# Feed-forward gate products of a two-layer block: the high weights meet high and low rows in one matmul of 512 columns

## The chip, the cores and the metric

The kernel runs on one core of one Trainium2 chip. The metric is device time in microseconds (us) of one launch; three runs of the kernel before gave 1533.83, 1536.38 and 1536.64 us, median 1536.38 us.

## The reference, cut to what matters

A sequence of 256 tokens with 1024 features goes through two layers. Each layer is feed-forward, token mixing (window attention, a gated recurrence and gated linear attention), feed-forward; each part reads a normalised and modulated copy of x and adds its output to x. Shift, scale and gate come from nine vectors per layer, products of a condition vector with w_ada (1024 x 9216 per layer). All is float32. The part that changes is the first product of the four feed-forwards:

```
def swiglu(h, w_i, w_o):                       # h: 256 x 1024, w_i: 1024 x 5632, w_o: 2816 x 1024
    a, g = jnp.split(h @ w_i, 2, axis=-1)
    return (jax.nn.silu(g) * a) @ w_o
h = modulate(rms_norm(x, norm_g[l, 0]), sh1, sc1)
x = x + 0.5 * g1[:, None, :] * swiglu(h, w_ff_in[l, 0], w_ff_out[l, 0])
```

## The kernel before, in words

Activations are held transposed: 128 features on the partitions, 256 tokens along the row, in C = 8 chunks. Every weight slab is 128 x 2048 floats (eight chunks of 128 x 256). The precision of float32 comes from splitting: ScalarE copies the raw slab to a rounded high part (`hi`, line 1015), VectorE subtracts to get the low part (`lo`, line 1494), and TensorE computes high x high, high x low and low x high, each as a matmul of 256 moving columns (`slab_tile`, line 503). A product of one slab is 2 output tiles x 8 chunks x 3 = 48 matmuls into the two halves of one PSUM bank. There are 240 slabs; three slots hold split slabs, so `hi` of slab p waits until slab p - 3 has been multiplied. SyncE loads the raw slabs into four slots.

A feed-forward handles 11 blocks of 256 hidden features, called rounds 0 to 10 here (`j` in the code); the four feed-forwards are called F1 to F4 (norms 0, 2, 3 and 5 in the code). TensorE's order in a round j is: gate product of block j+1 (bank 4), down product of block j (banks 0 to 3, 48 matmuls), up product of block j+1 (bank 5). In the last two rounds up 10 comes before down 9. ScalarE applies Silu to bank 4 (line 1088), VectorE multiplies by bank 5 (line 1633), ScalarE rounds the result (line 1111), VectorE takes its low part (line 1637), and only then may the down product begin. The order of each engine is written out by hand:

- VectorE in round j: `lo` of gate j+1; multiply j; `lo` of down j; low part of hidden j; `lo` of up j+1; then `weigh` (below). The next round begins with `lo` of gate j+2.
- ScalarE in round j: `hi` of gate j+1; `hi` of down j; high part of hidden j; `hi` of up j+1; Silu of gate j+1.
- TensorE waits for `lo` of a slab before its product, for Silu j before gate j+1 (bank 4 is used again), and for multiply j before up j+1.

Beside this, VectorE computes the modulation vectors: `weigh` multiplies and adds four 128 x 512 pieces of w_ada (lines 1384 and 1390), `fold_block` transposes and reduces every second one (lines 1401 and 1405). How many halves a round gets is a table, `FF_HALVES = [0, 2, 2, 1, 1, 1, 1, 2, 2, 0, 0]`; F4 has only the first four halves, in rounds 1 and 2. TensorE finishes the vectors in `ada_group` (line 601, bank 7): one at round 8, and in F1 to F3 a second one in round 9, after gate 10 and before up 10, which waits until VectorE has copied out the first (`ada_columns`, line 1414, in round 9 after `lo` of down 9). In F1 VectorE also has small operations of a series in rounds 1 to 8 (lines 1444 to 1470).

The first gate and up products of F2 to F4 (`lead`, banks 4 to 7) and gate 1 (`rows_halves`) have their own forms, and so have those of F1 (`stage`). In the opening, the first blocks of modulation (`ada`, line 587) go to banks 6 and 7 in turn.

Of the kernel before, what the change touches and what calls it, by code (L numbers as in the profile page):

```python
# [8 lines left out]
F32R = mybir.dt.float32r  # L9
# [5 lines left out]
P = 128  # L15
DEPTH = 2
D = 1024
T = 256
# [87 lines left out]
def build(nc, x, c, w_ada, b_ada, norm_g, w_ff_in, w_ff_out, w_in, qk_norm_g, attn_sinks, rel_bias,  # L106
# [3 lines left out]
    with ctx:  # L110
# [3 lines left out]
        def sem(name):  # L114
# [12 lines left out]
        h_hi, h_lo = sb("h_hi", [C, T], F32R), sb("h_lo", [C, T], F32R)  # L127
# [89 lines left out]
         consts_ready, bias_masked, fold_ready, ada_folded, ma_ready, mhi_ready, mlo_ready, xhi_ready, xlo_ready, lead_scaled, c_loaded, small_loaded, x_loaded, c_turned, turned, x_turned, par_ready, lam_ready, lam_exp,  # L217
# [10 lines left out]
             "consts_ready bias_masked fold_ready ada_folded ma_ready mhi_ready mlo_ready xhi_ready xlo_ready lead_scaled c_loaded small_loaded x_loaded c_turned turned x_turned par_ready lam_ready lam_exp "  # L228
# [60 lines left out]
        def ff_groups(l, f):  # L289

            first, blocks = ff_ada(l, f)
            return [(first, min(blocks, 4))] + ([(first + 4, blocks - 4)] if blocks > 4 else [])

# [198 lines left out]
        def _(pe):  # L492
# [22 lines left out]

            def rows_halves(p, bank, norm):
# [55 lines left out]
            def ada(b):  # L572
# [3 lines left out]
                if b >= 2:  # L576
                    pe.wait_ge(ada_saved, b - 1)
# [4 lines left out]
                for t in range(4):  # L582
                    to, cols = ps[:, 6 + b % 2, t:t + 1], slice(t * P, (t + 1) * P)
# [56 lines left out]
            for l in range(DEPTH):  # L640
# [26 lines left out]
                def ff(f, q):  # L667
# [23 lines left out]
                    if norm == 0:  # L691
# [4 lines left out]
                        stage(up_in[0], 5, *STAGES[0])  # L696
                        for p, bank in ((gate_in[0], 4), (up_in[0], 5)):
                            stage(p, bank, *STAGES[1])
                        ada(3)
                        stay_busy(0, 3)  # L700
                        for p, bank in ((gate_in[0], 4), (up_in[0], 5)):
                            stage(p, bank, *STAGES[2])
# [3 lines left out]
                    for j in range(NF):  # L706
# [4 lines left out]
                        elif j + 1 < NF:  # L711
                            pe.wait_ge(silu_ready, n + 1)
                            product(gate_in[j + 1], 4, (h_hi, h_lo))
                        if j == 8:
                            ada_group(*ff_groups(l, f)[0])
                        if j + 2 == NF:
# [3 lines left out]
                            product(up_in[j + 1], 5, (h_hi, h_lo))  # L720
                        out_block(down[j], j, n + 1, final=j + 1 == NF)
                        if j + 2 < NF:
                            pe.wait_ge(hid_made, n + 1)
                            product(up_in[j + 1], 5, (h_hi, h_lo))
# [228 lines left out]
        def _(act):  # L953
# [51 lines left out]
            for l in range(DEPTH):  # L1005
# [57 lines left out]
                def ff(e, q):  # L1063
# [22 lines left out]
                    def silu(p):  # L1086
                        act.wait_ge(slab_done, p + 1)
                        f(t512a[:, :], ps[:, 4, :], ACT.Silu).then_inc(silu_ready, 1)  # L1088

                    if l == 0 and e == 0:  # L1090
                        silu(gate_in[0])
                    for j in range(NF):
# [19 lines left out]
                        if j + 1 < NF:  # L1112
                            hi(down[j] if j + 2 == NF else up_in[j + 1])
                            silu(gate_in[j + 1])
# [239 lines left out]
        def _(dve):  # L1354
# [63 lines left out]
            def ada(b):  # L1418

                dve.wait_ge(ada_done, b + 1)  # L1420
                if 0 < b < ADA_START // 2:
# [3 lines left out]
                    else:  # L1425
                        cp(pairs[:, :, 2 * b:2 * b + 2],
                           ps[:, 6 + b % 2, 0:4].rearrange("p (v k) -> p v k", v=2)).then_inc(ada_saved, 1)
# [556 lines left out]
```

## Time and profile before

| | |
|---|---|
| median of three runs | 1536.38 us |
| profiled execution, its own time | 1537.28 us |
| its span (first to last instruction of the program) | 1535.5 us |
| around the span | 1.8 us |
| TensorE matmul busy | 1500.9 us, 98% |
| TensorE weight load busy | 1459.2 us, 95% |
| VectorE busy | 1140.1 us, 74% |
| ScalarE busy | 800.0 us, 52% |

Matmuls overlap each other in the rows: the duration of one (0.28 us) is its way through the engine, and what it costs in a stream is the distance from its start to the start of the next. An instruction that shows no idle time before it began as soon as the one before it on its engine let it.

### The profile page before, as it was taken

How to read it: one execution, taken by the hardware profiler on the slowest of the kernel's cores; microseconds unless marked ns; L12 is line 12 of the kernel's file. 1: busy time of each engine (PE TensorE's matmuls, PEld its weight loads, DVE VectorE, ACT ScalarE, POOL GpSimd, SP SyncE). 2: the span in 40 equal slices, each digit the busy share in tenths (PEclk: the TensorE clock that was granted, in tenths of full speed). 3: DMA queues.
4: the chain of work that ended last, by engine and by line, in shares of the span. 5: the costliest groups of instructions: out<-in, count | busy, mean ns of one | idle time of the engine just before them, and what ended most of it. 6: DMA issues, size and time to landing. Idle time of an engine off the chain costs nothing.

```text
span 1535.5 us, 29169 instructions
## 1 busy us (share of the span) xinstructions
PE 1500.9 (98%) x12530; PEld 1459.2 (95%) x12530; DVE 1140.1 (74%) x1547; ACT 800.0 (52%) x970; POOL 25.3 (2%) x29
## 2 busy tenths in 40 slices
PE   5999999999999999999999999999999999999999
PEld 4999999999999999999999999999999999999998
DVE  6597777898546998776877768769965589977454
ACT  4344337888546446433464434677955544464342
POOL 0000000000100000000000000000001000000000
PEclk8899999999999999999999999999999999999999
DMA  9989855554456895778658785454454599676551
GB/s 324 320 256 278 277 179 160 151 155 154 140 165 229 299 321 194 267 271 293 204 201 280 266 294 177 145 172 145 144 165 143 173 312 334 222 256 200 172 187 61
DMA packets 287345, 333.52 MB, mean 217 GB/s; under 512 B 13100, under 2 KB 241616, under 8 KB 287216
## 3 DMA queue, kind: packets, MB, share of 16 engines
q1 hardware_dynamic: 279456, 327.40, 65.2%
q10 hardware_dynamic: 7760, 4.26, 1.2%
q8 instruction: 99, 1.62, 0.4%
q14 instruction: 30, 0.25, 0.1%
HBM read 330.23 MB, written 1.38 MB: 216 GB/s over the span
## 4 chain that ended last, share of the span: by engine, by line
PE 78%; DVE 12%; ACT 7%; issue 2%; DMA 1%; ACTq 0%; SPq 0%; DVEq 0%
PE ps L503 67%; DVE w_lo L1494 4%; PE ps L889 3%; ACT w_hi L1015 2%; DVE scratch L1390 2%; DVE hf L1551 1%; DVE h_lo L1556 1%; PE ps L804 1%; PE ps L587 1%; DVE xT L1571 1%; PE ps L762 1%; ACT L1028 1%; ACT xm L1041 1%; PE ps L751 1%; PE ps L817 1%
## 5 line engine op out<-in xcount | busy, mean ns | idle before, releaser
L503 PE MATMUL ps<-h_hi,w_hi 128*128 128x256 f32 x2320 | 654.7, 282 | 1.0 <-DVE w_lo L1494 1.0
L503 PE MATMUL ps<-h_lo,w_hi 128*128 128x256 f32 x2320 | 644.7, 278 | 0.0
L503 PE MATMUL ps<-h_hi,w_lo 128*128 128x256 f32 x2320 | 643.3, 277 | 0.0
L1494 DVE TENSOR_TENSOR w_lo<-raw,w_hi 128x2048 fp32r<-128x2048 f32 x238 | 543.7, 2286 | 113.8 <-ACT w_hi L1015 113.8
L1015 ACT ACTIVATE w_hi<-raw 128x2048 fp32r<-128x2048 f32 x237 | 452.5, 1912 | 202.4 <-PE ps L503 197.0
L503 PEld LDWEIGHTS ps<-h_hi,w_hi 128*128 128x128 f32 x2320 | 435.1, 188 | 9.0 <-issue 6.7
L503 PEld LDWEIGHTS ps<-h_lo,w_hi 128*128 128x128 f32 x2320 | 438.8, 189 | 0.5 <-issue 0.5
L503 PEld LDWEIGHTS ps<-h_hi,w_lo 128*128 128x128 f32 x2320 | 435.1, 188 | 0.0
L503 PE MATMUL ps<-xm,w_hi 128*128 128x256 f32 x1408 | 251.2, 281 | 0.0
L503 PEld LDWEIGHTS ps<-xm,w_hi 128*128 128x128 f32 x1408 | 215.4, 189 | 0.0
L503 PE MATMUL ps<-xm,w_lo 128*128 128x256 f32 x704 | 197.4, 280 | 0.0
L1390 DVE SCALAR_TENSOR_TENSOR scratch<-eyr,cond,scratch 128x512 f32<-128x512 f32 x248 | 186.4, 752 | 9.7 <-DMA eyr<-in_w_ada_dram 0.6
L503 PEld LDWEIGHTS ps<-xm,w_lo 128*128 128x128 f32 x704 | 133.0, 189 | 0.0
L1633 DVE TENSOR_TENSOR t512b<-t512a,ps 128x512 f32<-128x512 f32 x41 | 28.2, 687 | 141.2 <-issue 83.6
L503 PE MATMUL ps<-hid_hi,w_hi 128*128 128x256 f32 x384 | 108.8, 283 | 1.6 <-DVE hid_lo L1637 1.5
L503 PE MATMUL ps<-hid_lo,w_hi 128*128 128x256 f32 x384 | 106.6, 278 | 0.0
L503 PE MATMUL ps<-hid_hi,w_lo 128*128 128x256 f32 x384 | 106.4, 277 | 0.0
L503 PEld LDWEIGHTS ps<-hid_hi,w_hi 128*128 128x128 f32 x384 | 72.0, 188 | 2.2 <-DVE w_lo L1494 1.8
L503 PEld LDWEIGHTS ps<-hid_lo,w_hi 128*128 128x128 f32 x384 | 72.7, 189 | 0.1
L503 PEld LDWEIGHTS ps<-hid_hi,w_lo 128*128 128x128 f32 x384 | 72.0, 187 | 0.0
L1088 ACT ACTIVATE t512a<-ps 128x512 f32<-128x512 f32 x41 | 24.5, 597 | 86.1 <-PE ps L503 83.4
L1111 ACT ACTIVATE xm<-t512b 128x512 fp32r<-128x512 f32 x20 | 12.7, 634 | 88.7 <-DVE t512b L1633 88.7
(270 smaller groups left out, 1639.2 us busy)
## 6 DMA issues: line engine op xcount, KB each, us to landing
raw<-in_w_ff_in_dram SPq DMA_DIRECT2D x176, 512.0 KB, 5.0
eyr<-in_w_ada_dram SPq DMA_DIRECT2D x144, 512.0 KB, 7.2
raw<-in_w_in_dram SPq DMA_DIRECT2D x100, 512.0 KB, 4.8
raw<-in_w_ff_out_dram SPq DMA_DIRECT2D x88, 512.0 KB, 4.8
raw<-in_w_gate_dram SPq DMA_DIRECT2D x48, 512.0 KB, 4.6
raw<-in_w_branch_dram SPq DMA_DIRECT2D x48, 512.0 KB, 4.6
raw<-in_w_out_dram SPq DMA_DIRECT2D x16, 512.0 KB, 5.9
rgw<-in_rg_w_dram ACTq DMA_DIRECT2D x16, 128.0 KB, 2.7
```

What stands on the lines that cost most here:

```text
L503: last = mm(outs, a, b[:, cc, :], start=clear and cc == 0 and q == 0, stop=cc == n - 1 and q == 2, skip_group_check=True)
L587: last = mm(to, acc[:, cols], ones[:, 0:1], start=not direct, stop=True)
L751: last = nc.tensor.transpose(ps[:, 4 + hh, b * P:(b + 1) * P], pr[:, hh, b * P:(b + 1) * P], ident[:, :])
L762: last = mm(ps[64 * r:64 * r + 64, 4 + 2 * t + m, 384:512], vtok[:, half, v], prT[:, 2 * t + r, (m + half) * P:(m + half + 1) * P], start= ...
L804: last = mm(ps[:, 2 - g, t * T:(t + 1) * T], rgw[:, g, t, :], xc[:, t, :], start=True, stop=True)
L817: last = mm(ps[:, 4 + 2 * t + r, to], qn[rows, t, q], kk[rows, t, k], start=True, stop=True)
L889: last = mm(ps[:, 1, m * T:(m + 1) * T], a, b, start=cc == 0 and q == 0, stop=cc == C - 1 and q == 2)
L1015: f(w_hi[:, p % SPLIT, :], raw[:, p % RAW, :], ACT.Copy).then_inc(hi_ready, 1)
L1088: f(t512a[:, :], ps[:, 4, :], ACT.Silu).then_inc(silu_ready, 1)
L1390: ins = stt(acc, w[:, cc, :], by, acc, ALU.mult, ALU.add)
L1494: tt(w_lo[:, p % SPLIT, :], raw[:, p % RAW, :], w_hi[:, p % SPLIT, :].bitcast(F32), ALU.subtract).then_inc(lo_ready, 1)
L1633: tt(t512b[:, :], t512a[:, :], ps[:, 5, :], ALU.mult).then_inc(hid_made, 1)
```

## The change

The high and the low rows become one tile, `h_split` (2 x 8 x 256), in which `h_hi` and `h_lo` are views. Gate products 1 to 10 of F1 and 2 to 10 of F2 to F4 (`gate_is_wide`) are done by `wide_product`: for each of two output tiles and eight chunks one matmul of the high weights with 512 moving columns (256 high, 256 low) into a whole bank (4 or 5), and one of the low weights with the 256 high columns into the first half of that bank. So 32 matmuls stand in the place of 48, in two banks in the place of one. The sum of the two halves is made outside TensorE: ScalarE copies the low halves of both banks to `t512a`, VectorE adds the high halves, ScalarE applies Silu to the sum in place. Up products move from bank 5 to bank 6, and the opening blocks of modulation share bank 7, so `ada(1)` waits until `ada(0)` has been copied out.

```diff
+        def gate_is_wide(norm, j):
+            return j > (1 if norm else 0)
...
+            def wide_product(p, bank):
+                pe.wait_ge(lo_ready, p + 1)
+                for t in range(2):
+                    for cc in range(C):
+                        w = [slab_kn(b, p % SPLIT)[:, cc, t * P:(t + 1) * P] for b in (w_hi, w_lo)]
+                        mm(ps[:, bank + t, :].rearrange("p (b t) -> p b t", b=2), w[0], h_split[:, :, cc, :], start=cc == 0,
+                           stop=False, skip_group_check=True)
+                        last = mm(ps[:, bank + t, 0:T], w[1], h_hi[:, cc, :], start=False, stop=cc == C - 1,
+                                  skip_group_check=True)
+                last.then_inc(slab_done, 1)
...
-                if b >= 2:
-                    pe.wait_ge(ada_saved, b - 1)
+                if b >= 1:
+                    pe.wait_ge(ada_saved, b if b < ADA_START // 2 else b - 1)
...
                             pe.wait_ge(silu_ready, n + 1)
-                            product(gate_in[j + 1], 4, (h_hi, h_lo))
+                            wide_product(gate_in[j + 1], 4)
...
-                    def silu(p):
-                        act.wait_ge(slab_done, p + 1)
-                        f(t512a[:, :], ps[:, 4, :], ACT.Silu).then_inc(silu_ready, 1)
+                    def low_copied(to, bank, signal):
+                        f(to[:, :].rearrange("p (a t) -> p a t", a=2), ps[:, bank:bank + 2, T:2 * T], ACT.Copy).then_inc(signal, 1)
+                    def silu(j):
+                        act.wait_ge(slab_done, gate_in[j] + 1)
+                        if gate_is_wide(3 * l + q, j):
+                            low_copied(t512a, 4, gate_low_copied)
+                            act.wait_ge(gate_added, gates_added(3 * l + q, j))
+                            f(t512a[:, :], t512a[:, :], ACT.Silu).then_inc(silu_ready, 1)
+                        else:
+                            f(t512a[:, :], ps[:, 4, :], ACT.Silu).then_inc(silu_ready, 1)
...
                         if j + 2 == NF:
                             lo(down[j])
+                        if j + 1 < NF and gate_is_wide(3 * l + q, j + 1):
+                            dve.wait_ge(gate_low_copied, gates_added(3 * l + q, j + 1))
+                            both = t512a[:, :].rearrange("p (a t) -> p a t", a=2)
+                            tt(both, ps[:, 4:6, 0:T], both, ALU.add).then_inc(gate_added, 1)
                         if j == 9:
                             ada_columns(*ff_groups(l, e)[0])
```

## Rows read from the trace of the kernel before

**Rows 1.** The page: busy shares, granted clock, chain of waits, costliest group.

```profile
PE 1500.9 (98%) x12530; PEld 1459.2 (95%) x12530; DVE 1140.1 (74%) x1547; ACT 800.0 (52%) x970; POOL 25.3 (2%) x29
...
PEclk8899999999999999999999999999999999999999
...
PE 78%; DVE 12%; ACT 7%; issue 2%; DMA 1%; ACTq 0%; SPq 0%; DVEq 0%
...
L503 PE MATMUL ps<-h_hi,w_hi 128*128 128x256 f32 x2320 | 654.7, 282 | 1.0 <-DVE w_lo L1494 1.0
```

**Rows 2.** Busy time by stretch, F2 round 5; columns: stretch, length, engines (instructions), clock.

```profile
693.28:709.90 16.62, 16.62 (x144) 16.62 (x143) 10.55 (x9) 6.76 (x5) 0.00 (x0) 1.00 0.76 267
```

**Rows 3.** Timeline, TensorE: other widths; columns: start, length, engine, line, operation.

```profile
51.23 0.81 PE L593 MATMUL ps<-kraw 128*128 128x512 bf16 x3
...
289.13 1.47 PE L751 MATMUL ps<-ident,pr 128*128 128x128 f32 x12
...
589.36 1.13 PE L648 MATMUL ps<-hf,ones 128*128 128x256 f32 x4 [1.14 <-ACT hf L1039]
```

**Rows 4.** Timeline, VectorE, F2 rounds 7 to 9.

```profile
729.01 0.69 DVE L1633 TENSOR_TENSOR t512b<-t512a,ps 128x512 f32<-128x512 f32 x1 [4.25 <-issue]
...
742.07 2.28 DVE L1494 TENSOR_TENSOR w_lo<-raw,w_hi 128x2048 fp32r<-128x2048 f32 x1
745.88 0.69 DVE L1633 TENSOR_TENSOR t512b<-t512a,ps 128x512 f32<-128x512 f32 x1 [1.53 <-issue]
746.49 2.29 DVE L1494 TENSOR_TENSOR w_lo<-raw,w_hi 128x2048 fp32r<-128x2048 f32 x1
...
751.50 0.48 DVE L1384 TENSOR_SCALAR scratch<-eyr,cond 128x512 f32<-128x512 f32 x1
...
758.94 4.48 DVE L1494 TENSOR_TENSOR w_lo<-raw,w_hi 128x2048 fp32r<-128x2048 f32 x2
...
768.73 0.71 DVE L1414 COPY mod<-ps 32x16 f32<-32x16 f32 x4
```

**Rows 5.** Timeline, ScalarE, F2 round 8.

```profile
751.37 0.60 ACT L1088 ACTIVATE t512a<-ps 128x512 f32<-128x512 f32 x1 [2.33 <-PE ps L503]
```

**Rows 6.** Timeline, TensorE, F2 rounds 8 and 9.

```profile
745.51 0.28 PE L503 MATMUL ps<-h_hi,w_lo 128*128 128x256 f32 x1
745.63 0.28 PE L503 MATMUL ps<-h_hi,w_hi 128*128 128x256 f32 x1
...
751.06 0.28 PE L503 MATMUL ps<-h_hi,w_lo 128*128 128x256 f32 x1
...
762.51 0.28 PE L503 MATMUL ps<-h_hi,w_hi 128*128 128x256 f32 x1
...
769.59 0.38 PE L601 MATMUL ps<-scratch,fold 128*128 128x32 f32 x2 [1.38 <-DVE mod L1414]
769.81 0.37 PE L503 MATMUL ps<-h_hi,w_hi 128*128 128x256 f32 x1
```

**Rows 7.** Timeline, VectorE's multiply in F1 (rounds 2, 3, 8) and F2 (round 3).

```profile
91.44 0.69 DVE L1633 TENSOR_TENSOR t512b<-t512a,ps 128x512 f32<-128x512 f32 x1 [1.46 <-issue]
...
108.08 0.69 DVE L1633 TENSOR_TENSOR t512b<-t512a,ps 128x512 f32<-128x512 f32 x1 [0.30 <-issue]
...
192.16 0.69 DVE L1633 TENSOR_TENSOR t512b<-t512a,ps 128x512 f32<-128x512 f32 x1 [0.87 <-issue]
...
661.99 0.69 DVE L1633 TENSOR_TENSOR t512b<-t512a,ps 128x512 f32<-128x512 f32 x1 [1.30 <-issue]
```

**Rows 8.** Timeline, TensorE, first matmuls of gate 4 in F1.

```profile
107.92 0.36 PE L503 MATMUL ps<-h_hi,w_hi 128*128 128x256 f32 x1
108.11 0.28 PE L503 MATMUL ps<-h_lo,w_hi 128*128 128x256 f32 x1
```

**Rows 9.** Timeline, opening: VectorE's copy of `ada(1)`, and TensorE's first product.

```profile
26.57 0.16 DVE L1424 COPY mod<-ps 128x4 f32<-128x4 f32 x1 [1.54 <-PE ps L587]
...
30.48 0.36 PE L547 MATMUL ps<-h_hi,w_hi 128*128 128x256 f32 x1 [1.37 <-ACT h_hi L1061]
```

More of the change, by code:

```diff
@@ L126, in build @@
         sb("place_h", [32])
-        h_hi, h_lo = sb("h_hi", [C, T], F32R), sb("h_lo", [C, T], F32R)
+        h_split = sb("h_split", [2, C, T], F32R)
+        h_hi, h_lo = h_split[:, 0, :, :], h_split[:, 1, :, :]
         hid_hi, hid_lo = sb("hid_hi", [2, T], F32R), sb("hid_lo", [2, T], F32R)
@@ L292, in ff_groups, with gates_added, ada_bank @@
             return [(first, min(blocks, 4))] + ([(first + 4, blocks - 4)] if blocks > 4 else [])
+        def gate_is_wide(norm, j):
+            return j > (1 if norm else 0)
+        def gates_added(norm, j):
+            before = (0, None, NF - 1, 2 * NF - 3, None, 3 * NF - 5)[norm]
+            return before + (j if norm == 0 else j - 1)
+        def ada_bank(b):
+            return 7 if b < ADA_START // 2 else 6 + b % 2
         def pair_group(l):
@@ L582, in ada @@
                 for t in range(4):
-                    to, cols = ps[:, 6 + b % 2, t:t + 1], slice(t * P, (t + 1) * P)
+                    to, cols = ps[:, ada_bank(b), t:t + 1], slice(t * P, (t + 1) * P)
                     if direct:
@@ L695, in ff @@
                         ada(2)
-                        stage(up_in[0], 5, *STAGES[0])
-                        for p, bank in ((gate_in[0], 4), (up_in[0], 5)):
+                        stage(up_in[0], 6, *STAGES[0])
+                        for p, bank in ((gate_in[0], 4), (up_in[0], 6)):
                             stage(p, bank, *STAGES[1])
@@ L700, in ff @@
                         stay_busy(0, 3)
-                        for p, bank in ((gate_in[0], 4), (up_in[0], 5)):
+                        for p, bank in ((gate_in[0], 4), (up_in[0], 6)):
                             stage(p, bank, *STAGES[2])
@@ L719, in ff @@
                             pe.wait_ge(hid_made, n + 1)
-                            product(up_in[j + 1], 5, (h_hi, h_lo))
+                            product(up_in[j + 1], 6, (h_hi, h_lo))
                         out_block(down[j], j, n + 1, final=j + 1 == NF)
@@ L723, in ff @@
                             pe.wait_ge(hid_made, n + 1)
-                            product(up_in[j + 1], 5, (h_hi, h_lo))
+                            product(up_in[j + 1], 6, (h_hi, h_lo))
                 ff(0, 0)
@@ L1113, in ff @@
                             hi(down[j] if j + 2 == NF else up_in[j + 1])
-                            silu(gate_in[j + 1])
+                            silu(j + 1)
                 ff(0, 0)
@@ L1426, in ada @@
                         cp(pairs[:, :, 2 * b:2 * b + 2],
[L1427 removed]
+                           ps[:, ada_bank(b), 0:4].rearrange("p (v k) -> p v k", v=2)).then_inc(ada_saved, 1)
                     return
                 at = 4 * (b % ADA_BLOCKS)
[L1430 removed]
+                cp(mod[:, b // ADA_BLOCKS, at:at + 4], ps[:, ada_bank(b), 0:4]).then_inc(ada_saved, 1)
             def lam_before():
@@ L1632, in ff @@
                         else:
-                            tt(t512b[:, :], t512a[:, :], ps[:, 5, :], ALU.mult).then_inc(hid_made, 1)
+                            tt(t512b[:, :], t512a[:, :], ps[:, 6, :], ALU.mult).then_inc(hid_made, 1)
                         if j + 2 < NF:
```

7 lines of the change are left out of this document (3 added, 4 removed).

## The prediction

> **What bounds the kernel now.** I read the page first: busy shares, granted clock, chain of waits [rows 1]. TensorE is busy 98% of the span, at the higher granted clock from the fifth slice on, and 78% of the chain that ended last is TensorE's. Next I wanted the price of a matmul in a stream, which the mean duration (282 ns) is not. In the stretch table a quiet round of F2 holds 144 matmuls in 16.62 us without a gap: 115.4 ns each, 5.54 us for a product of 48 [rows 2]. Last I read the timelines of the three engines, since the change gives VectorE and ScalarE work in every round. In the quiet round VectorE is busy 10.55 of 16.62 us and ScalarE 6.76: both have room [rows 2]. In a heavy round, one with two halves of `weigh`, VectorE works without a pause from one multiply to the end of the next gate slab's `lo`, and only 1.53 us are idle before the next multiply [rows 4]. So TensorE sets the pace everywhere, but in the heavy rounds VectorE is about one microsecond behind it. The reader is to see that there: this small rest decides what the change is worth.
>
> **The gain on TensorE.** A triple of 256-column matmuls costs 3 x 115.4 = 346 ns. In its place stand one of 512 columns and one of 256. No row shows the first in this data type. Three bf16 matmuls of 512 columns run 0.215 us apart ((0.81 - 0.38)/2, the last two starts), and four fp32 passes of 256 columns, each with its own weight load, about 0.216 us apart [rows 3]: an operand stream of 213 ns at the full clock plus 2 to 3 ns, with the weight load hidden beneath it. At 256 columns the stream would be 107 ns, but the pace is 115.4; twelve matmuls of 128 columns run 0.109 us apart ((1.47 - 0.27)/11), so it is the weight load that lies just under the pace, and 512 columns hide it [rows 3]. Bounds for the pair: 215 + 109 = 324 ns below, where both matmuls run at their floors; 2 x 115.4 + 115.4 = 346 ns above, where cost goes by column alone. A little worse than that is possible if reading high and low rows from one tile costs more. I take 216 + 115.4 = 331.4 ns, since the narrow one still has a weight load as long as itself: 14.8 ns saved per triple, 16 triples a product, 0.24 us a product; 10 + 3 x 9 = 37 products, 8.8 us in all. The ends are 0 and 37 x 16 x 22 ns = 13 us.
>
> The Trainium skill, TensorE: Matmul & The Clock Gate, section "Back-to-back issue gap", has two figures for 512 columns: about 216 ns isolated, and about 131 ns in a stream with weight loads, because "at large N it over-counts". The rows above have 512 columns 215 ns apart, back to back, so by them the first figure holds. What the second would make of the time is a rival below.
>
> **What is added.** A copy on ScalarE (priced as Silu of the same size, 0.60 us [rows 5]), an add on VectorE (as the multiply, 0.69 us, of which the next instruction sees 0.61 [rows 4]), and the Silu after it. Silu j+1 is then some 1.4 us later, but TensorE wants it a down and an up product later, 11 us: free. ScalarE's `hi` of the next gate slab is 1.4 us later too; in quiet rounds VectorE's room covers that. What is queued behind the new wait on VectorE is `weigh`, and behind that `lo` of the next gate slab, for which TensorE waits. So I follow one heavy round in time from its multiply, M (M = 745.88) [rows 4 to 6]:
> - Last matmul of the up product at M - 0.37, first of the gate product at M - 0.25, last at M + 5.18, Silu at M + 5.49 (0.31 after). With the gate product 0.24 shorter the copy runs from M + 5.25 to 5.85 and the add can start at M + 5.90.
> - VectorE began `weigh` at M + 5.62. Now it waits 0.28 for the copy and then adds for 0.61: 0.89 us later.
> - `lo` of the next gate slab ended at M + 15.34 (729.01 to 742.07 + 2.28); now M + 16.23. The next multiply was at M + 16.87 and would be at M + 16.63. TensorE needs `lo` about 0.15 us before the gate product's first matmul, and once it has had to wait, the second matmul is 0.08 late: with `lo` ending at 107.78 the first starts at 107.92, the second 0.19 after it instead of 0.116 [rows 7, 8]. So TensorE can go on at M + 16.38, its due time, plus 0.08.
>
> Rounds 1 and 7 therefore just fit: they cost 16.7 instead of 16.87, a gain of about 0.09 (round 1, whose rest is 1.46 [rows 7] and not 1.53) and 0.15 where it should be 0.24. Rounds 2 and 8 begin with VectorE already late, and then the distance from `lo` to `lo` is what counts: from L, the end of one gate slab's `lo`, the gate product's last matmul comes at L + 0.23 + 5.19, the copy ends 0.91 later, the add lets `weigh` begin at L + 6.99, and from there to the next L it is 15.34 - 5.62 = 9.72: 16.71 us. Round 2 took 16.64 (91.44 to 108.08 in F1 [rows 7], the same in F2): a loss of 0.07. Round 8 took 16.88 with its `ada_group`: a gain of 0.17.
>
> Round 9 of F1 to F3 holds the largest cost. TensorE stands before `ada_group` for 1.38 us until VectorE's `ada_columns` (768.73 to 769.44), which now comes behind the add [rows 4, 6]. L was 761.22 there, gate 10 began 1.29 later and up 10 at 769.81, L + 8.59. VectorE is the chain here (it had reached `lo` of down 9 later than ScalarE's copy would be ready, L + 6.33), so up 10 comes at L + 8.59 + 0.61 = L + 9.20. Gate 10 now begins in effect at L + 0.23. From gate 10 to up 10: before 769.81 - 762.51 = 7.30, after 8.97, a loss of 1.67, and the shorter gate product saves nothing.
>
> F1 has its small series besides. Idle before its multiply in rounds 3 and 8 is 0.30 and 0.87 us, against 1.30 and 1.53 in F2 [rows 4, 7], so `lo` ends 1.00 and 0.66 later. Round 2 becomes 17.71 instead of 16.82 (16.64 and the 0.18 that TensorE loses already): a loss of 0.89. In round 7 `lo` ends at M + 15.34 + 0.65 + 0.89 = M + 16.88; TensorE starts 0.23 after that, M + 17.11, due before at M + 16.62: a loss of 0.49.
>
> In the opening `ada(1)` on TensorE waits for VectorE's copy of `ada(0)` (0.16 us and two hand-overs, 0.3 us by the rows' spacing). VectorE waits for it (1.54 us idle), and TensorE's first product waits on that chain [rows 9]: a loss of 0.3. The bank numbers cost nothing.
>
> **The sum**, in us, minus is a gain. F2 and F3, each: rounds 1, 2, 7, 8: -0.09 + 0.07 - 0.15 - 0.17 = -0.34; quiet rounds 3 to 6: 4 x -0.24 = -0.96; round 9: +1.67; together +0.37. F1: round 0 -0.24, then -0.09 + 0.89 - 0.96 + 0.49 - 0.17 + 1.67, together +1.59. F4, quiet from round 3 on and without the second `ada_group`: -0.09 + 0.07 - 7 x 0.24 = -1.70. Opening +0.30. Total 1.59 + 0.74 - 1.70 + 0.30 = +0.9. On the profiled execution's 1537.28 that is 1538.2; its time lies 0.90 over the median of the runs, so I set 1537.3 beside 1536.38.
>
> 34 of the 37 products pass their gain on (not the three gates 10 before the stall), so with s saved a product the total is 0.93 + 34 x (0.24 - s): -3.1 at s = 0.355, +9.1 at s = 0.
>
> **The rivals.**
> 1. *The add slips in at 0.61 us, not 0.89.* If the copy is over when VectorE has finished `lo`, heavy rounds keep up with TensorE. F2 and F3: 8 x -0.24 and +1.46 in round 9, -0.46 each; F1 about +0.6; F4 -2.16; opening +0.3: -2.2, 1534.2. For it: the margin is 0.28 us. Against it: the copy can't start before the product's end.
> 2. *That, and the pair at its floor of 324 ns.* Another 34 x 0.115 = 3.9: 1530.3. For it: 109 ns between weight-loading matmuls. Against: no 256-column stream runs under 115.
> 3. *512 columns cost twice 256.* Place: all 592 wide matmuls. Then nothing is saved on TensorE and all that was added stays: +9.1, 1545.5. It decides from a pair of about 335 ns, where the total passes +3.07. For it: this data type has not been seen at 512 columns, and its pace at 256 is 8 ns over the stream. Against: the fp32 passes.
> 4. *VectorE's lateness costs more than a place in the queue.* Each late `lo` pushes later `hi`, loads and `weigh` too; with 0.4 us more in each of the 14 heavy rounds +6.5, 1542.9. For it: F1's round 3, where TensorE did wait. Against: it lost only 0.18 there.
> 5. *A stream of 512 columns paced by the weight load alone.* If a wide matmul overlapped the next and cost little more than the 115.4 of a narrow one, a product would save 16 x 100 ns = 1.6 us; the 20 quiet products keep it, 1507 or so. For it only the section of TensorE: Matmul & The Clock Gate in the Trainium skill that is named above, with its 131 ns. Against: 215 ns in rows 3.
>
> **How the numbers follow.** 0.2% is 3.1 us, about what a measurement can tell from no change. Chances: the forecast 0.47, rival 1 0.14, rival 2 0.12, rival 3 0.14, rival 4 0.11, rival 5 0.02. Rival 2, rival 5 and the lower edge of the forecast and rival 1 (0.06) give faster 0.20; rivals 3 and 4 and the forecast's upper edge (0.03) give slower 0.28; the same 0.52. The range takes in rival 2 nearly and rival 4, and stops before rival 3's end: 1531.5 to 1543.5.
>
> **What would show it.** In the profile after: wide matmuls 216 ns from the next start and the narrow ones 115, a quiet round of 16.4 us; VectorE idle about 0.3 us before the add; in heavy rounds no idle time before the multiply (or next to none) and TensorE 16.7 us a round; the wait before the second `ada_group` grown from 1.4 to about 3 us; first product at 30.8. The forecast is wrong if the pair is under 325 or over 335 ns, or if heavy rounds come out at 16.4 us.

## The result, and the profile after

The changed kernel takes 1554.36 us (median of four runs, 1552.06 to 1555.09) against 1536.41 us before: ratio 1.0111, 95% interval 1.0098 to 1.0123, slower by 17.9 us between the medians and by 17.1 by the ratio. The forecast was 1537.3 and the range ended at 1543.5. The profiled execution took 1552.06 us with a span of 1550.3, 14.8 more than before; the places below are found in it. One of the ten runs of banks_only below took 1841.89 us, at a mean granted clock of 0.75 against 0.99 in the others, and is left out of its ratio.

First the page of the changed kernel, the answer to [rows 1]: busy shares, granted clock, chain, and the two groups of the wide gate products (partitions x elements, count, busy us and mean ns of one).

```profile
PE 1512.5 (98%) x11938; PEld 1444.7 (93%) x11938; DVE 1164.8 (75%) x1584; ACT 823.7 (53%) x1007; POOL 25.2 (2%) x29
...
PEclk8899999999999999999999999999999999999999
...
PE 78%; DVE 12%; ACT 6%; issue 2%; DMA 1%; ACTq 0%; SPq 0%; DVEq 0%
...
L536 PE MATMUL ps<-h_split,w_hi 128*128 128x512 f32 x592 | 207.9, 391 | 1.3 <-DVE w_lo L1529 1.3
...
L538 PE MATMUL ps<-h_split,w_lo 128*128 128x256 f32 x592 | 165.3, 279 | 0.0
```

There are 592 matmuls fewer, and TensorE is busy 11.6 us *longer*. The streams show it. Here is one quiet round of F2 in the changed kernel by stretch, cut at the last matmul of each product: down 4, up 5, gate 6 (columns as in [rows 2]).

```profile
689.59:695.25 5.66, 5.66 (x50) 5.66 (x49) 5.04 (x8) 3.04 (x3) 0.00 (x0) 1.00 1.02 356
695.25:700.90 5.65, 5.65 (x51) 5.65 (x49) 2.67 (x2) 1.92 (x1) 0.00 (x0) 1.00 0.79 247
700.90:706.45 5.55, 5.55 (x35) 4.89 (x34) 5.18 (x4) 2.44 (x2) 0.00 (x0) 1.00 0.39 143
```

The gate product, 32 matmuls now, takes 5.55 us: as long as the 48 took [rows 2]. And the down and up product beside it, whose instructions the change left alone, take 5.65 (in every second round; the others kept their 5.74 and 5.59). So there are two losses: a gain that isn't there, and a price on neighbours (the products beside the wide one). The timeline of TensorE in that gate product:

```profile
704.83 0.39 PE L536 MATMUL ps<-h_split,w_hi 128*128 128x512 f32 x1
705.06 0.28 PE L538 MATMUL ps<-h_split,w_lo 128*128 128x256 f32 x1
705.18 0.39 PE L536 MATMUL ps<-h_split,w_hi 128*128 128x512 f32 x1
705.40 0.28 PE L538 MATMUL ps<-h_split,w_lo 128*128 128x256 f32 x1
705.52 0.39 PE L536 MATMUL ps<-h_split,w_hi 128*128 128x512 f32 x1
```

From wide start to wide start 0.34 to 0.35 us; over the product 228.5 ns for the wide one and 118.4 for the narrow one, 346.9 ns a pair (one wide and one narrow matmul). The triple (three narrow ones) cost 346. The forecast had 331.4.

VectorE in heavy rounds 7 to 9 of F2, the answer to [rows 4]:

```profile
751.88 0.69 DVE L1668 TENSOR_TENSOR t512b<-t512a,ps 128x512 f32<-128x512 f32 x1 [0.42 <-issue]
...
758.08 0.69 DVE L1681 TENSOR_TENSOR t512a<-ps,t512a 128x512 f32<-128x512 f32 x1 [0.51 <-ACT t512a L1114]
...
766.13 4.48 DVE L1529 TENSOR_TENSOR w_lo<-raw,w_hi 128x2048 fp32r<-128x2048 f32 x2
770.53 0.68 DVE L1668 TENSOR_TENSOR t512b<-t512a,ps 128x512 f32<-128x512 f32 x1
...
775.92 0.68 DVE L1681 TENSOR_TENSOR t512a<-ps,t512a 128x512 f32<-128x512 f32 x1
776.52 0.71 DVE L1449 COPY mod<-ps 32x16 f32<-32x16 f32 x4
```

The rest of 1.53 us before the multiply [rows 4] is down to 0.42, the add waits 0.51 for ScalarE's copy, and in round 9 the add stands right ahead of `ada_columns`, for which TensorE waits. TensorE there, against [rows 6]:

```profile
774.21 0.28 PE L538 MATMUL ps<-h_split,w_lo 128*128 128x256 f32 x1
777.38 0.38 PE L627 MATMUL ps<-scratch,fold 128*128 128x32 f32 x2 [2.89 <-DVE mod L1449]
777.60 0.48 PE L517 MATMUL ps<-h_split,w_hi 128*128 128x256 f32 x2
```

The wait grew from 1.38 to 2.89 us. What it set off is in the stretch table: round 9 from that wait on, in F1, F2 and F3 (the clock is the third column from the end; the third stretch is cut otherwise, it begins before the wait and ends within up 10).

```profile
216.17:226.64 10.47, 7.58 (x51) 7.34 (x50) 6.75 (x17) 3.25 (x4) 0.00 (x0) 0.84 0.58 154
774.21:783.22 9.01, 6.12 (x52) 5.87 (x50) 6.64 (x17) 3.25 (x4) 0.00 (x0) 1.00 0.62 196
967.00:976.50 9.50, 6.61 (x32) 6.24 (x32) 7.05 (x16) 3.35 (x4) 0.00 (x0) 0.69 0.50 118
```

In F2 the clock stays, and up 10 ends 9.01 us after gate 10. In F1 and F3 the clock is at the lower level (1.2 GHz) for part of the product behind the wait, and from gate 10's last matmul to up 10's it takes 10.47 and 11.82 us (967.86 to 979.68).

The 14.8 us by product, from the last matmul of one to the last of the next: 34 down and up products at +0.105, 3.6; up 10 in F1 to F3 3.07, 1.60 and 4.40, 9.1; gates 4 and 9 in F1 0.89 and 0.72, 1.6; other gates 0.9; the mixing and F4's up 10 0.4; the opening 0.9 less. The only gate product that got shorter is gate 2 of F3, 5.65 to 5.55 us, and there the kernel before was the one that ran at the slower pace.

### The profile page after: what moved, and what is told of

Same layout as the page of the kernel before. It is cut to its first block, busy times and chain, and to the rows that moved or that the text cites. A ratio compares the mean times of both kernels' runs of the same rounds, so it can differ in the third digit from the quotient of the medians.

```text
span 1550.3 us, 28060 instructions
## 1 busy us (share of the span) xinstructions
PE 1512.5 (98%) x11938; PEld 1444.7 (93%) x11938; DVE 1164.8 (75%) x1584; ACT 823.7 (53%) x1007; POOL 25.2 (2%) x29
## 3 DMA queue, kind: packets, MB, share of 16 engines
HBM read 330.23 MB, written 1.38 MB: 214 GB/s over the span
## 4 chain that ended last, share of the span: by engine, by line
PE 78%; DVE 12%; ACT 6%; issue 2%; DMA 1%; ACTq 0%; SPq 0%; DVEq 0%
PE ps L517 54%; PE ps L536 8%; DVE w_lo L1529 4%; PE ps L538 4%; PE ps L915 3%; ACT w_hi L1041 2%; DVE scratch L1425 2%; DVE hf L1586 1%; DVE h_split L1591 1%; PE ps L830 1%; PE ps L613 1%; DVE xT L1606 1%; PE ps L573 1%; PE ps L788 1%; ACT L1054 1%
## 5 line engine op out<-in xcount | busy, mean ns | idle before, releaser
L517 PE MATMUL ps<-h_split,w_hi 128*128 128x256 f32 x3456 | 618.3, 282 | 1.0 <-DVE w_lo L1529 1.0
L517 PEld LDWEIGHTS ps<-h_split,w_hi 128*128 128x128 f32 x3456 | 528.1, 189 | 9.5 <-issue 7.2
L517 PE MATMUL ps<-h_split,w_lo 128*128 128x256 f32 x1728 | 481.4, 279 | 0.0
L517 PEld LDWEIGHTS ps<-h_split,w_lo 128*128 128x128 f32 x1728 | 326.0, 189 | 0.0
L536 PE MATMUL ps<-h_split,w_hi 128*128 128x512 f32 x592 | 207.9, 391 | 1.3 <-DVE w_lo L1529 1.3
L538 PE MATMUL ps<-h_split,w_lo 128*128 128x256 f32 x592 | 165.3, 279 | 0.0
L536 PEld LDWEIGHTS ps<-h_split,w_hi 128*128 128x128 f32 x592 | 111.2, 188 | 25.1 <-issue 1.7
L538 PEld LDWEIGHTS ps<-h_split,w_lo 128*128 128x128 f32 x592 | 110.8, 187 | 0.0
```

What stands on the lines that cost most here:

```text
L517: last = mm(outs, a, b[:, cc, :], start=clear and cc == 0 and q == 0, stop=cc == n - 1 and q == 2, skip_group_check=True)
L536: mm(ps[:, bank + t, :].rearrange("p (b t) -> p b t", b=2), w[0], h_split[:, :, cc, :], start=cc == 0, stop=False, skip_group_check=True)
L538: last = mm(ps[:, bank + t, 0:T], w[1], h_hi[:, cc, :], start=False, stop=cc == C - 1, skip_group_check=True)
```

## The experiments

Times are against the kernel before on the same chip, 1536.3 to 1537.0 us in every batch.

**m1_streams.** The disputed cost alone: streams of matmuls with nothing beside them. float32r is the type of the rounded high and low tiles.

```
def A256():      mm(ps[:, 4, 0:256], w(n), h[:, 0, n % 8, :])             # x48
def C512two():   mm(ps[:, 6, :] as 2 x 256, w(n), h[:, :, n % 8, :])      # x48
def I_triple():  hi*hi, hi*lo, lo*hi, 256 columns each                    # x72
def H_pair():    hi*(hi,lo) with 512 columns, lo*hi with 256              # x48
def L_bf512(), M_bf256(): the same in bf16
```

> Only streams of matmuls on slabs loaded once, each form 48 times (the triple and the pair 24 times); nothing of the reference is computed. Theory A (float32r matmuls cost by the column, about 0.447 ns each at the high clock, whatever their width): start to start about 115 to 118 ns at 256 columns, 143 at 320, 171 at 384, 228 at 512, in one run or in two; narrowing the weights to 64 columns changes nothing; pair and triple both about 347 ns; bf16 213 to 216 at 512. Theory B (the two runs of 256 columns, 8 KB apart, cost the 512-column matmul its last 13 ns): 512 in one run 215 to 217, in two runs 228. Theory C (the weight load and the moving stream get in each other's way): with 64 weight columns 512 falls to 213 to 220 and 256 to under 112. Rows that start 8 bytes off a 32-byte line: about 120 to 122 ns at 256 columns if the start address is what makes odd down products slower (5.74 against 5.55 us), 115 to 118 if not. After a pair stream the triple should run flat at 118 ns, before it at 115.6, if the pair leaves its mark on what follows.

Stretches from the first matmul of one stream to that of the next: 512 columns in one run and in two (48 matmuls each), 384, 320, the triple (72), the pair (48), bf16 of 512 and of 256 (48 each).

```profile
42.21:53.12 10.91, 10.91 (x51) 9.02 (x50) 0.00 (x0) 0.00 (x0) 1.00 0.00 0
53.12:63.99 10.87, 10.87 (x49) 9.01 (x48) 0.00 (x0) 0.00 (x0) 1.00 0.01 2
63.99:72.34 8.35, 8.35 (x49) 8.34 (x48) 0.00 (x0) 0.00 (x0) 1.00 0.00 0
72.34:79.37 7.03, 7.03 (x49) 7.02 (x49) 0.00 (x0) 0.00 (x0) 1.00 0.01 2
101.63:110.27 8.64, 8.64 (x75) 8.64 (x73) 0.00 (x0) 0.00 (x0) 1.00 0.00 0
110.27:118.75 8.48, 8.48 (x51) 7.35 (x49) 0.00 (x0) 0.00 (x0) 1.00 0.01 2
133.11:143.48 10.37, 10.37 (x50) 4.71 (x49) 0.00 (x0) 0.00 (x0) 1.00 0.00 0
143.48:148.64 5.16, 5.16 (x49) 4.62 (x48) 0.00 (x0) 0.00 (x0) 1.00 0.00 0
```

The mean distance from start to start is the price of one (a stretch divided by its count comes within 0.3 ns of it, but for the last, which ends early): float32r 256 columns 120.0 ns, 320 146.5, 384 173.9, 512 227.3 and 226.7; bf16 109.1 at 256 and 216.0 at 512. Taking off the columns at 2.4 GHz (106.7, 133.3, 160, 213.3) leaves 13.3, 13.2, 13.9 and 14.0 or 13.4 for float32r and 2.4 to 2.7 for bf16. So where the operands lie in this run, a float32r matmul carries 13 to 14 ns at each of the four widths; m2_places and m3_history show that this part moves with the place.

The same weights in all 48, loaded anew for each all the same, or the same rows change nothing at 512 columns once the stream runs steadily (227, 226.7). With 64 weight columns in place of 128 a matmul of 256 takes 113.5 ns, but one of 512 takes 230.2: no theory had that.

Pair 353 ns (8.48 / 24), triple 360: one matmul fewer saves 7 ns in place of 14.8, from a triple that is slower than the layer's 346, and the pair costs 7 ns more than its two matmuls do in streams of their own (226.7 + 120.0). The triple ran at 120.0 ns a matmul before the pair and behind it: no mark of the pair here.

The Trainium skill, TensorE: Matmul & The Clock Gate, section "Back-to-back issue gap", gives N / 2.4 + 2.5 ns: the bf16 streams agree, the float32r ones are 11 ns above it, and its 131 ns for 512 columns is in no stream here.

**narrow_halves.** The change with the wide matmul taken apart; banks, copy and add stay.

```diff
-mm(ps[:, bank + t, :].rearrange("p (b t) -> p b t", b=2), w[0], h_split[:, :, cc, :], start=cc == 0, ...)
+mm(ps[:, bank + t, 0:T], w[0], h_hi[:, cc, :], start=cc == 0, stop=False, ...)
+mm(ps[:, bank + t, T:2 * T], w[0], h_lo[:, cc, :], start=False, stop=False, ...)
```

> The changed kernel with each wide matmul taken apart again: high rows into columns 0 to 255, low rows into 256 to 511 of the bank, 48 matmuls a product; copy, add and Silu stay. Theory A (width saves nothing, the loss comes from the added copy and add): within 3 us of the changed kernel, 1551 to 1557. Theory D (the wide form itself slows the products that follow it, 0.106 us each in even rounds): 3.5 to 4.5 us less than the changed kernel, about 1550, and those products back at 5.55 us. If the wide matmul had been a gain hidden by other losses: 1557 or more.

1551.43 us, ratio 1.0098 (1.0081 to 1.0115): 2.9 us less than with the wide matmul, just under the 3.5 to 4.5 that theory D asked for (F2 has a third fall of the clock here, which costs 1.6). The same three products as above, in this kernel:

```profile
690.27:695.81 5.54, 5.54 (x50) 5.54 (x49) 4.94 (x8) 3.04 (x3) 0.00 (x0) 1.00 1.00 343
695.81:701.36 5.55, 5.55 (x50) 5.55 (x49) 2.77 (x2) 1.92 (x1) 0.00 (x0) 1.00 0.78 259
701.36:706.91 5.55, 5.55 (x51) 5.55 (x50) 5.18 (x4) 2.44 (x2) 0.00 (x0) 1.00 0.42 151
```

Gate 6 is as long with 48 narrow matmuls as with 32, and down and up are back at 5.55. So the neighbours' price, in the rounds where the change has it, comes with the wide matmul, not with the banks or VectorE's traffic. But 5.65 is not found behind wide matmuls alone: down 8, up 9 and gate 10 of F1 and down 2 and up 3 of F4 run 0.1 us longer in this kernel too, and the kernel before has 5.65 at up 1 and gate 2 of F3. Up 10 costs 3.0 to 3.2 us more than before in all of F1 to F3, each with a fall of the clock.

**wide_only.** The reverse: wide matmuls, no copy and no add (the product of high weights and low rows is left out of the sum).

```diff
-low_copied(t512a, 4, gate_low_copied)
-act.wait_ge(gate_added, gates_added(3 * l + q, j))
-f(t512a[:, :], t512a[:, :], ACT.Silu)...
+f(t512a[:, :].rearrange("p (a t) -> p a t", a=2), ps[:, 4:6, 0:T], ACT.Silu)...
...
-tt(both, ps[:, 4:6, 0:T], both, ALU.add).then_inc(gate_added, 1)
```

> The changed kernel without copy and add: Silu reads the high halves of the two banks directly, so the high-weight by low-row part is left out of the gate. All that TensorE does stays. Theory A: the waits in rounds 2, 3, 8 and 9 and both falls of the clock go, and what is left over the kernel before is the opening's 0.3 us and the slower neighbours, so 1536.7 to 1541. If VectorE's and ScalarE's added work caused the slower neighbours too: 1537 and neighbours at 5.55 us. If the loss lay in TensorE's work: over 1545.

1540.14 us, 1.0022 (1.0013 to 1.0032), within theory A's 1536.7 to 1541. With nothing added, the wide matmul alone makes the kernel 3.4 us slower by the ratio: nothing gained and 34 x 0.105 = 3.6 lost on neighbours (they take 5.65 here too). The two halves are nearly additive: 0.0022 + 0.0098 (narrow_halves) = 0.0120 over 1, and the change has 0.0111.

**contig_rows.** High and low rows of a chunk side by side, so that the 512 columns are one run.

```diff
-h_split = sb("h_split", [2, C, T], F32R)
+h_split = sb("h_split", [C, 2, T], F32R)
```

> The changed kernel with high and low rows of a chunk side by side, so that the 512 moving columns are one run. Theory B (two runs cost 13 ns): a wide matmul falls from 228 to 216 ns, about 34 x 16 x 12 ns = 6.5 us less than the changed kernel, 1548. Theory A: no change, 1551 to 1557.

1553.33 us, 1.0107 (1.0092 to 1.0123): the same as the change. The two runs of columns are not the cause. Its profiled execution (1553.74 us against the change's 1552.06) has a fall of the clock in round 9 of all of F1 to F3.

**banks_only.** The banks alone: up in 6, opening blocks in 7, products as before.

```diff
-wide_product(gate_in[j + 1], 4)
+product(gate_in[j + 1], 4, (h_hi, h_lo))
```

> The kernel before with only the bank numbers and the opening's wait of the change: up products in bank 6, opening blocks in bank 7. Prediction's term: +0.3 us from the opening, so 1536.6; neighbours at 5.55 us. If the banks slow even rounds' products by 0.106 us each: 1540.

1536.92 us, 1.0001 (0.9992 to 1.0011). Nothing, and so no 0.3 us in the opening that a run could tell either.

**wide_early** and **early_columns.** Round 9's wait taken away at its root: `ada_columns` goes from behind the add to right behind multiply 9, in the changed kernel and in the kernel before.

```diff
+                        if j == 9:
+                            ada_columns(*ff_groups(l, e)[0])      # behind the multiply
...
-                        if j == 9:
-                            ada_columns(*ff_groups(l, e)[0])
```

> The changed kernel with ada_columns of round 9 moved from behind the add to right behind multiply 9. If round 9's wait (1.6 us longer than before) and the fall of the clock after it (1.5 us each) are what the profile shows, both go in F1 to F3, and the wait of 1.4 us that the kernel before had goes too: 1554.4 - 3 x (3.1 + 1.4) = about 1541. If the falls of the clock come from something else: 1545. If VectorE's lateness merely moves to up 10: 1550 or more.

> The kernel before with the same move alone: no wide products. If VectorE's idle 0.70 us before the low part of hidden 9 hides the four copies, TensorE's 1.4 us before the second ada_group goes in F1 to F3: about 4.5 us less than before, 1531.8. If something else is late there: 1536.

wide_early: 1543.97 us, 1.0045 (1.003 to 1.006), 10.4 us under the change. early_columns: 1532.61 us, 0.9969 (0.9956 to 0.9981), up 10 1.63 us shorter in each of F1 to F3. VectorE in early_columns, round 9 of F2: the copies go into the pause before the low part of hidden 9, which [rows 4] did not list.

```profile
760.91 0.68 DVE L1633 TENSOR_TENSOR t512b<-t512a,ps 128x512 f32<-128x512 f32 x1
761.50 0.72 DVE L1414 COPY mod<-ps 32x16 f32<-32x16 f32 x4
762.29 0.69 DVE L1639 TENSOR_TENSOR xm<-t512b,xm 128x512 fp32r<-128x512 f32 x1
```

And in wide_early, from gate 10's last matmul through up 10 and on into down 9 (76 matmuls), where the change took 9.01 us with 2.89 idle for up 10 alone:

```profile
773.20:782.00 8.80, 8.80 (x76) 8.76 (x75) 6.09 (x12) 3.04 (x3) 0.00 (x0) 1.00 0.63 203
```

No wait, no fall. By product, wide_early saves 4.59, 3.13 and 5.94 us at up 10 (13.7), of which 1.7 come back at the down 10 that follow, 2.3 at the first products of what comes next, and 2.1 in the opening, which no edit touched (see below); the two profiles differ by 7.7 and the medians by 10.4. Up 10 takes 5.88 us in it and 5.78 in early_columns, so the 13.7 are the wait that the kernel before had too (4.9, early_columns), the lateness (3 x 1.60, taken to be in F1 and F3 what it is in F2) and the clock (4.3), less these 0.3. No run shows the half clock in round 9 once the wait is gone.

**m2_places.** Since neighbours had changed pace without changing, the question was what sets it. The triple and the pair in streams, at sixteen places of the rows (`h`) and of the low weights (`l`), in floats past a multiple of 64.

```
h = hs[:, A:A + 4096]; w_lo = w_lows[:, B:B + 2048]     # A, B in 0, 16, 32, 48; then triple x72, pair x48
```

> Only streams of 24 triples and 24 pairs on slabs loaded once, with the rows and the low weights shifted by 0, 64, 128 or 192 bytes against each other (16 combinations of each form); nothing of the reference is computed. Theory E (a float32r matmul pays a fixed 13.3 ns over its columns; the triple's 8.9 ns in the kernel is a better case given by where its operands lie): the triple moves between 347 and 360 ns with the place, and the pair does not fall under 347. Theory F (place has no part in it): triple 360 and pair 356 everywhere. If some place brings the pair to 331, a wide product could still pay.

Stretches: triple and pair at h16 l0, at h16 l48 (the kernel's place) and at h16 l16.

```profile
53.28:61.44 8.16, 8.16 (x74) 8.16 (x73) 0.00 (x0) 0.00 (x0) 1.00 0.00 0
61.44:69.92 8.48, 8.48 (x51) 7.38 (x49) 0.00 (x0) 0.00 (x0) 1.00 0.01 2
...
120.45:128.92 8.47, 8.47 (x74) 8.47 (x73) 0.00 (x0) 0.00 (x0) 1.00 0.00 0
128.92:137.24 8.32, 8.32 (x50) 7.33 (x49) 0.00 (x0) 0.00 (x0) 1.00 0.01 2
187.95:196.43 8.48, 8.48 (x74) 8.48 (x73) 0.00 (x0) 0.00 (x0) 1.00 0.01 2
196.43:204.61 8.18, 8.18 (x51) 7.23 (x49) 0.00 (x0) 0.00 (x0) 1.00 0.00 0
```

Divided by 24: at h16 l0 the triple takes 340 ns and the pair 353, at the kernel's place 353 and 347, at h16 l16 353 and 341. (A mean over the start distances of such a stream, as the expectations have it, misses one narrow distance and puts the pair 2 to 3 ns higher.) Over all places the triple takes 340 to 360 ns and the pair 341 to 353: where one is fast the other is not, the best pair is no better than the best triple, and nowhere does the pair reach 331. Both go below the 347 that theory E had as their floor. Each place was run once and in one order, so place and what ran before are not told apart here. 347 is what the pair costs in the layer too; the triple there cost 346, not the 353 of this stream.

**low_at_0**, **early_low0**, **wide_early_low0.** The low weights moved to offset 0, as at h16 l0 above, in the kernel before, in early_columns and in wide_early.

```diff
-sb("place_low", [48])
-sb("place_h", [32])
+sb("place_h", [80])
```

> The kernel before with one edit: the low weight slabs begin 0 and not 192 bytes after a 1024-byte line (48 floats of padding moved from before them to before the rows, which stay where they were). The stream run had the triple at 113.4 ns a matmul in that place and at 117.7 in the kernel's. Theory E (place sets the fixed part of a float32r matmul): about 2.2 ns less than 115.6 on some 8,000 to 10,000 matmuls, an upper bound of 20 us; in heavy rounds VectorE becomes the limit, so 10 to 18 us less than before: 1519 to 1527. Theory F (the kernel's 115.6 has another cause): 1536 or more.

> The same place together with ada_columns behind multiply 9. If both add up: 4.4 us under low_at_0. If TensorE's faster pace leaves VectorE late in round 9 too: 2 to 4 us under it. This would be the version that beats both kernels.

> wide_early in the same place. In the stream run the pair was 355.6 ns there, the triple 340. Theory E: wide products cost 16 x 15 ns = 0.25 us more each than three narrow ones, 9 us over 37, and with copy and add 12 to 17 us more than early_low0. If the pair keeps its 347 ns in the kernel: 8 to 11 us more.

1543.08 us (1.0052, 1.0037 to 1.0067), 1539.1 (1.0019, 1.0009 to 1.0028) and 1546.14 (1.007, 1.0055 to 1.0085). Each is slower than its twin at the old place (by 6.8, 6.5 and 2.2 us), where the stream promised the two narrow ones a gain: most products ran at 5.65 us, and of 112 only up 1 and gate 2 of F2 at 5.44, the very next on the same slots at 5.65 again. wide_early_low0 is 7.0 us over early_low0, less than either expectation, and its wide gate products take 5.65 us like the narrow ones. This theory, that the offsets modulo 64 floats alone set the pace, fell.

**early_low0_h448.** As early_low0, with the padding ahead of the rows 32 floats longer (`place_h` 112 instead of 80; the expectation's 448). What is declared behind the rows, hidden tiles and `xm` among them, moves with them.

> early_low0 with the rows another 128 bytes on (448 bytes over the line). The stream run had the triple at 113.7 there, 113.4 in early_low0's place: the same time within 3 us by theory E. If only the one distance works in the kernel: 4 us or more slower than early_low0.

1522.87 us, ratio 0.9922 (0.9897 to 0.9947): 13.4 us faster than the kernel before by the medians, 12.0 by the ratio, and the best of both kernels and all trials. The expectation of the same time as early_low0 missed by 16. Down 4, up 5 and gate 6 of F2 in it:

```profile
681.25:686.69 5.44, 5.44 (x50) 5.44 (x49) 5.26 (x8) 2.41 (x2) 0.00 (x0) 1.00 1.01 342
686.69:692.13 5.44, 5.44 (x50) 5.44 (x49) 1.88 (x1) 1.92 (x1) 0.00 (x0) 1.00 0.99 345
692.13:697.57 5.44, 5.44 (x50) 5.44 (x49) 5.07 (x4) 2.45 (x2) 0.00 (x0) 1.00 0.28 90
```

48 matmuls in 5.44 us, 113.3 ns each: this is the pace the pair has to beat. F1 does not have it until up 9; its products still take 5.65 us and more, at the same places.

**wide_early_h448.** The same places with the wide gate products.

> The changed kernel with ada_columns behind the multiply, low weights at 0 and rows at 448 floats modulo 1024, to be compared with early_low0_h448 (1522.9 us), which is the same without the wide gate. Theory that a 512-column matmul keeps its own fixed 13 ns while the narrow triple has lost most of it there (5.44 us a product, 113.3 ns a matmul; pair 177.7 ns a matmul in the stream, 355 against 340 ns): gate products about 5.68 us, 37 x 0.24 = 9 us slower, with the late add and neighbours 12 to 17 us, 1535 to 1540 us. Rival, that the pair comes down with the triple: gate products 5.45 us and only VectorE's lateness left, 1525 to 1529 us.

1544.36 us, 1.0048 (1.0031 to 1.0065): 21.5 us slower than its narrow twin, more than either theory said (12 to 17, or 2 to 6). The same three products:

```profile
688.07:693.72 5.65, 5.65 (x49) 5.65 (x48) 4.95 (x8) 3.04 (x3) 0.00 (x0) 1.00 1.02 337
693.72:699.38 5.66, 5.66 (x51) 5.66 (x50) 2.67 (x2) 1.92 (x1) 0.00 (x0) 1.00 0.81 267
699.38:705.03 5.65, 5.65 (x35) 4.90 (x33) 5.28 (x4) 2.44 (x2) 0.00 (x0) 1.00 0.39 136
```

Wide gates cost 5.65 (353 ns a pair, as in the stream at this kind of place), 0.21 above the narrow ones, nearly as expected; not expected was that 23 ups and 9 downs behind them lose their fast pace too, 0.2 us each, 6.5 us. Its profile also has a stretch at the half clock from 1340.9 us on, which the twin's has not.

**m3_history.** The kernel's place held fixed, and only what ran before changed; then fewer weight columns.

```
t1 (triple x24), p1 (pair x24), t2 (triple), x1 (triple on rows with a pitch of 258 floats), t3 (triple), b1 (8 bf16), t4 (triple), p2, x2, t5
```

> A stream alone, its output is not the layer's. All operands lie at one place (the kernel's own offsets); only what ran before changes: 72 matmuls of the triple, then the pair (one of 512, one of 256 columns), then the triple again, triples on rows with a pitch of 258 floats, eight bf16 matmuls, and triples after each; last come 256 and 512 columns with 32, 64, 96 and 128 weight columns. If what ran before sets the pace: the triple runs at about 113 to 116 ns a matmul in one place of the sequence and at 117.8 or 120 in another. If only the places set it: all triples within 0.5 ns of each other, and the pairs too. If the weight load is in the fixed 13 ns: 256 columns fall from about 118 ns with 128 weight columns towards 107 with 32, and 512 from 227 towards 214. If it is not: all four widths of the weights within 1 ns.

Stretches of t1, t2 (behind p1, 24 pairs), t3 (behind x1); then 256 columns with 32 and with 128 weight columns (48 each).

```profile
44.76:53.23 8.47, 8.47 (x74) 8.47 (x73) 0.00 (x0) 0.00 (x0) 1.00 0.01 2
61.56:70.04 8.48, 8.48 (x74) 8.48 (x73) 0.00 (x0) 0.00 (x0) 1.00 0.00 0
78.67:87.00 8.33, 8.33 (x75) 8.29 (x73) 0.00 (x0) 0.00 (x0) 1.00 0.01 2
...
121.50:126.90 5.40, 5.40 (x50) 5.13 (x48) 0.00 (x0) 0.00 (x0) 1.00 0.00 0
171.56:177.30 5.74, 5.74 (x49) 5.74 (x48) 0.00 (x0) 0.00 (x0) 1.00 0.00 0
```

The same 72 instructions on the same addresses take 117.7 ns each in t1 and t2 and 115.7 in t3 (the stretch over 72); t4 and t5 have the distances of t3. Their starts are 118, 118, 117 apart in t1 and t2, and 112, 118, 116 in t3: the very patterns of the slowed and the unslowed products in the layer. So what ran before sets the pace, and it then keeps itself up. 8 bf16 matmuls between do not disturb it. That a pair brings the slow pace back is not shown here: t2 was slow before its pair too, and behind the second pair came x2, not a triple. The weight load has a part in the ns over the columns, but not all: from start to start 113.4 ns with 32 weight columns, 119.8 with 128, and with 512 columns 231.1 and 233.4. The last is the width that took 226.7 in m1_streams: its price moves too.

## Why the prediction was wrong

The step that failed is **the gain on TensorE**: "I take 216 + 115.4 = 331.4 ns". The pair costs 346.9. Both halves of the sum were low: the wide one is 228.5, not 216, and the narrow one 118.4, not 115.4. The 216 came from bf16 matmuls and fp32 passes [rows 3]; the 8 ns over the stream at 256 columns was put down to a weight load that 512 columns hide. m1_streams shows 13 to 14 ns at 256, 320, 384 and 512 columns alike, so width hides nothing. The rows did not say otherwise: the fp32 passes take 216 ns for 256 columns and 109 ns for 128, so both pay 0.83 ns a column (two cycles at 2.4 GHz) and 2 to 3 ns over. The 109 ns were read as a weight load's floor; by this reading, which no run tests on its own, they follow from the columns. At s = 0 (s is the gain per product) the prediction's own formula gives +9.1, rival 3's number, and its place (all wide matmuls) and its decision point (a pair over 335 ns) were right, for a reason it held against itself: this data type had not been seen at that width. The missing gain is 8.1 of the 17.1 us by which the forecast was off.

Two things were in no case, though both lay beyond rival 3:
- *Neighbours.* 3.6 us in the profile, 3.4 in wide_only. The prediction said of the wide matmul only what it would save; that instructions left alone could change pace was not thought of. The mean of 115.4 ns came from [rows 2], and its inner pattern of 112, 118 and 116 was not looked at.
- *The clock.* Behind the grown wait in round 9 the clock is at half in F1 and F3 here and in all three in narrow_halves, about 1.5 us each (10.47 against 9.01; 2.8 in F3 here); wide_early, without the wait, has no fall. The Trainium skill, TensorE: Matmul & The Clock Gate, section "What's actually happening", says that an idle array falls back to half its clock. The rows agree, 0.84 and 0.69, though F2's wait of the same length left 1.00, and the wait of 1.4 us before had cost nothing of this kind. The prediction had forecast the wait "about 3 us" and priced it as time alone.

Point by point, for the rest:
- Round 9, from gate 10's first matmul to up 10's: before 7.30, forecast 8.97, measured 8.81 in F2, where the clock held (the 1.60 above has 0.08 of up 10's own in it). Right.
- F1's round 2, from gate 3 to gate 4: 16.82 before, 17.93 after, +1.11; the forecast of +0.89 holds a gain of 0.24 and is +1.13 without it. Gate 9, 0.49 and the gain of 0.24 that would have hidden part: 0.73; measured 0.72. Right.
- The add's idle time, 0.28: 0.43 and 0.51. The copy was later by the pair's missing gain.
- Heavy rounds 1, 2, 7, 8 of F2, from gate to gate: with s = 0 the forecast is +0.15, +0.31, +0.09 and +0.07; measured +0.13, +0.31, +0.07 and +0.20. Right but for round 8, where the neighbours come on top. Rival 4 (0.4 us more in each heavy round) is out.
- The opening, +0.3: not seen; the profile has 0.9 the other way, and banks_only no difference. The term was within what the opening varies by: gate 1 of F1 ends at 63.1 us before and at 61.6 in early_columns, with the same opening, and at 62.2 in the change and 64.4 in wide_early, again with the same one.
- "No cost for the bank numbers": right, 1.0001.
- Rivals 1 and 2 needed a cheaper pair, rival 5 one far cheaper: none.

Adding up: the forecast +0.9, the missing gain 8.1, neighbours 3.6 and the clock 4.3 (1.46 + 2.81) make 16.9. The profiled executions differ by 14.8, of which the opening's 0.9 + 0.3 is on the other side. The 0.9 left over is mostly counted twice, by the times of the products: in round 2 VectorE sets the pace, and the forecast's +0.31 there already holds the 0.21 of the two neighbours, 0.85 in four feed-forwards. The medians differ by 17.9, because the profiled run of the kernel before lies 0.9 over its median and that of the change 2.3 under its own. narrow_halves and contig_rows, which have three falls of the clock in their profiles, suggest that the change's with two was a mild one, but no row shows the clock of the others by stretch (their means are 0.986 to 0.989, the profiled run's 0.989).

Open: why float32r carries 7 to 13 ns a matmul over its columns at 256 and 13 to 20 at 512, where bf16 has 2.4 to 2.7 (weight columns move it by 6 ns at 256 columns, by 2 at 512, and were not taken to none), and what switches the pace. m3_history shows that history does it at fixed places; early_low0 against early_low0_h448 shows that the place matters, in a kernel otherwise the same. No run says what lies behind either, and no run predicts the best place. The wide gate was no shorter than the narrow one at the kernel's place (5.55 both), at low0 (5.65 both) and at h448 (5.65 against 5.44); the place where the stream favours the pair (h16 l16, 341 against 353 ns) was not tried in the layer.

## What to carry to other kernels

Price an instruction in its own data type: a matmul's stream cost can have a part that more columns do not hide, and a stream of it alone (m1_streams) answers what the rows of another type can't. Price a TensorE wait that grows with a possible fall of the clock behind it, and put the waited-for copies into the first pause that will take them: early_columns is that alone, 4.8 us by its ratio. And when TensorE is busy 98%, compare the start distances of products that nothing touched; 48 matmuls in 5.44, 5.55 or 5.65 us are the same instructions, and the place of their operands, with what runs before, was worth 9.7 us here (early_low0_h448 against early_columns), more than any of the reordering.

## What the runs showed of the hardware

- float32r matmuls in a stream: in m1_streams columns at 2.4 GHz plus 13 to 14 ns (256: 120.0; 320: 146.5; 384: 173.9; 512: 226.7), bf16 plus 2.4 to 2.7 ns; elsewhere 113.3 at 256 (early_low0_h448) and 233.4 at 512 (m3_history).
- The 256-column triple has several steady paces, 113.3, 115.7, 117.7 and 120.0 ns a matmul among them, with fixed patterns of start distances. They change as operands move by 64 bytes (113.4 to 120.0 in m2_places) and with what ran before on the same addresses (115.7 or 117.7, m3_history).
- Products of 48 behind a wide gate product run at the slower of two paces: 5.65 instead of 5.55 us, and 5.65 instead of 5.44. That pace also comes without wide matmuls (up 1 and gate 2 of F3 in the kernel before).
- A wait of 2.89 us left the clock at full in F2, and waits as long were followed by the half clock in F1 and F3, at 1.5 and 2.8 us of time. After the three waits of 1.4 us of the kernel before it did not fall.
